# Staged first loads with zero products ahead of them, and last products in eight banks with a mean taken chunk by chunk

## What is computed

```python
h = rmsnorm(x, norm_mix[layer])                     # start: layer 0
z = jax.nn.gelu(h @ w_in)                           # start: first product
...
x = x + moe_swiglu(h, m_w_router[j], ...)           # end: expert rows added to x
return rmsnorm(x, norm_final), new_rows, win_state, jnp.stack(a_states)
```

## Time and profile before

| | us |
|---|---|
| three runs, median (lowest to highest) | 1208.33 (1204.21 to 1209.13) |
| the profiled execution, its own time | 1208.35 |
| its span in the trace | 1206.7 |
| PE busy | 1165.2 (97% of the span) |
| DVE busy | 800.0 |
| ACT busy | 694.8 |
| mean granted TensorE clock, share of full | 0.983 |

### The profile page before, as it was taken

The page is one execution under the profiler, slowest core; times in us unless marked ns, Lnnn a source line. Parts: engine busy times, 40 slices in busy tenths (PEclk is TensorE's granted clock), DMA queues, the critical chain, the costliest instruction groups (busy, mean ns, idle before and its releaser), DMA issues.

```text
span 1206.7 us, 20229 instructions
## 1 busy us (share of the span) xinstructions
PE 1165.2 (97%) x7512; PEld 946.0 (78%) x7512; DVE 800.0 (66%) x1257; ACT 694.8 (58%) x1081; POOL 52.8 (4%) x77
## 2 busy tenths in 40 slices
PE   6999999999999899999999999998999999999987
PEld 6999999999996678854888888655888887887544
DVE  6677666666653976402998997206998998996214
ACT  6666444555547787302887886105887887885011
POOL 1000000000430000100000000000000000000100
PEclk9999999999999899799999999999999999999997
DMA  9574545455666966999999999899999999998992
GB/s 348 185 260 181 200 158 201 158 201 209 236 205 221 384 207 262 410 393 382 420 421 421 392 421 383 346 420 420 420 420 422 421 423 358 404 418 316 389 420 84
DMA packets 69236, 390.36 MB, mean 323 GB/s; under 512 B 6710, under 2 KB 25786, under 8 KB 30682
## 3 DMA queue, kind: packets, MB, share of 16 engines
q1 hardware_dynamic: 64138, 367.44, 76.9%
q0 software_dynamic: 5008, 21.72, 5.0%
HBM read 366.92 MB, written 26.40 MB: 326 GB/s over the span
## 4 chain that ended last, share of the span: by engine, by line
PE 82%; DVE 7%; DMA 5%; ACT 4%; issue 2%; SPq 0%; DVEq 0%; ACTq 0%
PE bank L2229 12%; PE bank L2230 12%; PE bank L2231 12%; PE bank L1733 9%; PE bank L1734 9%; PE bank L1735 8%; PE bank L2180 8%; PE bank L2161 4%; DMA raw<-in_moe 4%; PE bank L2214 1%; DMA ring<-in_wd 1%; ACT arena L865 1%; PE bank L2094 1%; DVE d_lo L1147 1%; DVE w_lo L1582 1%
## 5 line engine op out<-in xcount | busy, mean ns | idle before, releaser
L1582 DVE TENSOR_TENSOR w_lo<-raw,w_hi 128x1024 fp32r<-128x1024 f32 x330 | 394.0, 1220 | 26.1 <-ACT w_hi L984 14.3
L984 ACT CAST w_hi<-raw 128x1024 fp32r<-128x1024 f32 x330 | 340.2, 1055 | 67.2 <-PE bank L2231 52.8
L1147 DVE TENSOR_TENSOR d_lo<-ring,d_hi 128x1024 fp32r<-128x1024 f32 x120 | 147.8, 1237 | 84.9 <-ACT d_hi L736 82.5
L1733 PE MATMUL bank<-hA_hi,d_hi 128*128 128x264 f32 x640 | 184.5, 288 | 12.4 <-DVE hA_lo L1137 9.5
L1734 PE MATMUL bank<-hA_lo,d_hi 128*128 128x264 f32 x640 | 182.4, 285 | 0.0
L1735 PE MATMUL bank<-hA_hi,d_lo 128*128 128x264 f32 x640 | 182.2, 285 | 0.0
L2229 PE MATMUL bank<-w_hi,xg_hi 128*128 128x512 f32 x440 | 172.7, 392 | 2.8 <-DVE w_lo L1582 2.8
L2230 PE MATMUL bank<-w_lo,xg_hi 128*128 128x512 f32 x440 | 172.1, 391 | 0.0
L2231 PE MATMUL bank<-w_hi,xg_lo 128*128 128x512 f32 x440 | 171.9, 391 | 0.0
L736 ACT CAST d_hi<-ring 128x1024 fp32r<-128x1024 f32 x120 | 125.0, 1045 | 77.5 <-PE bank L1735 68.6
L1733 PEld LDWEIGHTS bank<-hA_hi,d_hi 128*128 128x128 f32 x640 | 121.6, 190 | 14.8 <-issue 12.5
(11 more groups left out here) (372 smaller groups left out, 1717.1 us busy)
## 6 DMA issues: line engine op xcount, KB each, us to landing
raw<-in_moe SPq DMA_DIRECT2D x258, 1024.0 KB, 13.5
ring<-in_wd SPq DMA_DIRECT2D x29, 2048.0 KB, 8.1
out_rows<-zeros SPq DMA_DIRECT2D x1, 6656.0 KB
slot_rows<-zeros SPq DMA_DIRECT2D x1, 6144.0 KB
early_units<-in_moe SPq DMA_DIRECT2D x6, 1024.0 KB, 11.2
xs<-slot_rows POOLq DMA_DIRECT2D x5, 512.0 KB, 8.2
out_rows<-yrow POOLq DMA_DIRECT2D x5, 512.0 KB, 8.0
arena<-in_cmp_pages POOLq DMA_DIRECT2D x16, 128.0 KB, 3.2
```

What stands on the lines that cost most here:

```text
L984: nc.scalar.copy(w_hi[:, i % NSPLIT, :], raw[:, raw_slot(u), ITEM * (i % 2):ITEM * (i % 2) + ITEM])\
L1147: V.tensor_tensor(d_lo[:, n % NDS, :], raw_item(n), d_hi[:, n % NDS, :].bitcast(F32), ALU.subtract)\
L1582: V.tensor_tensor(w_lo[:, i % NSPLIT, :], raw[:, raw_slot(i // 2), ITEM * (i % 2):ITEM * (i % 2) + ITEM], w_hi[:, i % NSPLIT, :].bitcast(F ...
L1733: T.matmul(out, w_hi_[:, j, :], hi[:, k, :], start=(first and j == 0), stop=False)
```

## The change

At the start three waits are put between SP's issues: tile v0's rest waits for the second half of x, tile v1 for item 1, the constants and all behind them for tile v1. PE runs twelve matmuls of zeros (256 columns) before the first product. At the end `yrow` is copied in quarters, the eight products get eight banks and follow one another, the pairwise additions of squares are gone, the mean is taken of every chunk, `stay_awake` is gone from this part, and root and reciprocal are one instruction each.

```diff
-        LAST_BANKS = [T0, T1, B[0], B[1], STAT, T0, T1, B[0]]
+        LAST_BANKS = [T0, T1, B[0], B[1], B[3], STAT, MISC, B[2]]
...
             sp.wait_ge(item_in[0], 16)
             sp.dma_start(ring[:, 0, DITEM:2 * DITEM], wd[0][:, DITEM:2 * DITEM]).then_inc(item_in[1], 16)
+            sp.wait_ge(x_in[1], 16)
...
                     sp.dma_start(ring[:, n % NSLOT, first:], wd[wn][:, first:]).then_inc(done, 16)
                     wn += 1
+                if n == 0:
+                    sp.wait_ge(item_in[1], 16)
                 if n == NSLOT - 1:
 
+                    arrived(sp, TILES[n])
                     sp.dma_start(C[:], consts).then_inc(spatial_in, 16)
...
+            pe.wait_ge(zeros_ready, 1)
+            for _ in range(12):
+                T.matmul(MISC[:, 0:256], zeros[:, 0:P], zeros[:, :], start=True, stop=True)
             pe.wait_ge(setup_in, 16)
...
-            nc.scalar.copy(yrow[0:64, 0:512], B[2][0:64, :]).then_inc(left_ready, 1)
+            for half in range(2):
+                nc.scalar.copy(yrow[0:64, 256 * half:256 * half + 256], B[2][0:64, 256 * half:256 * half + 256]).then_inc(left_ready, 1)
...
-            nc.scalar.activation(tok_rstd[:, 0:2], B[2][:, 0:2], ACT.Sqrt, bias=vector("eps")[:, 0:1])
-            nc.scalar.activation(tok_rstd[0:NS, 2:3], B[2][0:NS, 2:3], ACT.Sqrt, bias=vector("eps")[0:NS, 0:1]).then_inc(tok_std, 1)
+            nc.scalar.activation(tok_rstd[:, 0:3], T0[:, 0:3], ACT.Sqrt, bias=vector("eps")[:, 0:1]).then_inc(tok_std, 1)
...
-            V.tensor_copy(yrow[64:128, 0:512], B[2][64:128, :]).then_inc(right_ready, 1)
-            for c in range(KC):
-                add_combined(1, c)
-                if c in (2, 4, 6, 7):
-                    j = c // 2 - 1 if c < 7 else 3
-                    dve.wait_ge(sq_ready, 32 + 2 * j + 2)
-                    V.tensor_tensor(sq_last[:, 2 * j, :], sq_last[:, 2 * j, :], sq_last[:, 2 * j + 1, :], ALU.add).then_inc(sum_step, 1)
+            for half in range(2):
+                V.tensor_copy(yrow[64:128, 256 * half:256 * half + 256], B[2][64:128, 256 * half:256 * half + 256]).then_inc(right_ready, 1)
+            for n in range(KC):
+                add_combined(1, n)
...
-            for c in range(KC):
-                combine(c)
-                if c >= 5:
-                    last_mean(c - 5)
-            last_mean(3)
-            stay_awake(B[3], 3)
-            pe.wait_ge(tok_scale, 4)
+            for n in range(KC):
+                combine(n)
+            for n in range(KC):
+                last_mean(n)
+            pe.wait_ge(tok_scale, 3)
```

More of the change, by code:

```diff
@@ L1690, in _ @@
             dve.wait_ge(yrow_free, wides + (WIDE_STEP + 1))
-            V.tensor_copy(yrow[64:128, 0:512], B[2][64:128, :]).then_inc(right_ready, 1)
-            for c in range(KC):
-                add_combined(1, c)
-                if c in (2, 4, 6, 7):
-                    j = c // 2 - 1 if c < 7 else 3
-                    dve.wait_ge(sq_ready, 32 + 2 * j + 2)
-                    V.tensor_tensor(sq_last[:, 2 * j, :], sq_last[:, 2 * j, :], sq_last[:, 2 * j + 1, :], ALU.add).then_inc(sum_step, 1)
+            for half in range(2):
+                V.tensor_copy(yrow[64:128, 256 * half:256 * half + 256], B[2][64:128, 256 * half:256 * half + 256]).then_inc(right_ready, 1)
+            for n in range(KC):
+                add_combined(1, n)
             dve.wait_ge(tok_std, 2)
-            V.reciprocal(tok_rstd[:, 0:2], tok_rstd[:, 0:2]).then_inc(tok_scale, 1)
-            V.reciprocal(tok_rstd[0:NS, 2:3], tok_rstd[0:NS, 2:3]).then_inc(tok_scale, 1)
+            V.reciprocal(tok_rstd[:, 0:3], tok_rstd[:, 0:3]).then_inc(tok_scale, 1)
             dve.wait_ge(rstd_spread, 1)
@@ L2122, in combine @@
             def combine(n):
[L2124 to L2128, removed]
+                if n in (0, 4):
+                    pe.wait_ge(left_ready, n // 4 + 1)
+                if n in (1, 5):
+                    pe.wait_ge(right_ready, n // 4 + 1)
+                if n == 5:
                     pe.wait_ge(comb_added, KC)
-                if n >= 5:
-                    pe.wait_ge(comb_added, KC + n - 4)
                 c = LAST_ORDER[n]
@@ L2135, in combine, with last_mean @@
                     .then_inc(comb_done, 1)
-            def last_mean(j):
-                stay_awake(B[3], 4 if j == 3 else 1)
-                pe.wait_ge(sum_step, 28 + j + 1)
+            def last_mean(n):
+                pe.wait_ge(sq_ready, 32 + n + 1)
                 for t, (a, z) in enumerate(spans):
-                    i = T.matmul(B[2][0:z - a, t:t + 1], sq_last[:, 2 * j, a:z], mean[:, 0:1], start=(j == 0 and t == 0), stop=(j == 3 and t == 2),
+                    i = T.matmul(T0[0:z - a, t:t + 1], sq_last[:, n, a:z], mean[:, 0:1], start=(n == 0 and t == 0), stop=(n == KC - 1 and t == 2),
                                  skip_group_check=True)
-                if j == 3:
+                if n == KC - 1:
                     i.then_inc(mean_done, 1)
```

## The result

The changed kernel took 1210.26 us in the median of 15 runs (1207.49 to 1214.37), the kernel before 1203.93 in the 15 runs beside it (1200.81 to 1209.13): ratio 1.0057, 95% interval 1.0042 to 1.0072, slower by 5 to 9 us. The forecast was 1204.5, 3.9 us faster than the profiled execution of before. A second set of 12 runs on another occasion gave 1209.85 against 1205.66, ratio 1.0031 (1.0010 to 1.0052).

The account below looks back on a forecast made before the run. PE, busy 97% of the span, was taken as the bound except at its two ends: item 1 and u0's arrival at the start, one token-wise mean at the end. 1208.35 - 0.7 - 3.1 = 1204.5 us, range 1201.6 to 1208.4.

Parts of the forecast that it names:

- Item 1 and product 2: Start: item 1 cast at 11.5 to 12.5 instead of 13.15, product 2 near 18.7 instead of 20.21.
- Zeros: Start of PE: twelve zero matmuls end near 9.8, product 0 then runs at full clock; no gain by itself.
- v1's landing: Start, loads: tile v1 lands at 18.9 instead of about 20.5, part of the engines' lag being gone.
- its 34.8: Start, loads: tile u0 lands at 34.8, as now; the queue loses about 1.8 us empty and regains the lag.
- only one wait finds the queue empty: Start, loads: of the added waits just one meets an empty queue and pays the fixed transfer cost of about 2 us.
- Rival 1: Start: u0 comes late, at 36.6, product 8 at 38.9, +1.0 us against now, time 1206.2; chance 0.2.
- the start term: Start up to product 8, at about 37.15 instead of 37.88: -0.7 us, bounds -1.6 and +1.0.
- The end: From the `yrow` copy to the scaling: -3.1 us, between -0.1 and -5.9; clock falling at about 1192.15 as now.
- -2.2 and -1.0: End: mean done at 1195.3 instead of 1197.53 (-2.2); root to scaling 2.0 instead of 2.99 us (-1.0).

Follow-up runs that it names:

- third_only: Kernel before plus only the wait of the constants and all behind them for tile v1; 1210.64 against 1205.66 us, ratio 1.0037.
- ctrl_after: The changed kernel run once more, nothing altered, against the kernel before; 1209.85 against 1205.66 us, ratio 1.0031.
- waits_only: Kernel before plus only the three waits between the first loads; 1212.83 against 1205.53 us, ratio 1.0049.
- after_filler: Changed kernel plus seven matmuls of zeros ahead of product 8, against the kernel before; 1206.80 against 1205.28 us, ratio 1.0028.
- ctrl_before: The kernel before run once more, nothing altered, against itself; 1202.93 against 1205.66 us, ratio 0.9974.
- tail_only: Kernel before with only the new last part, nothing changed at the start; 1204.04 against 1205.53 us, ratio 0.9982.
- tail_params_late: Kernel before with the new last part and parameters and late vectors issued behind tile u0, no waits or zeros; 1203.77 against 1205.28 us, ratio 0.9994.

## Why the prediction was wrong

The forecast was -3.8 us (-0.7 and -3.1) from the 1208.35 of one execution. In the first set the kernel before had a median of 1203.93, 4.4 us under that base, and the change came out at +6.3. So the change was missed by 10 us and the time by only 5.8, a piece of luck in the base.

**Item 1 and product 2: right.** Cast 11.40 (foreseen 11.5 to 12.5), product 2 at 18.45 (18.7). But the gain was counted against an execution in which item 1 happened to be late. Over the six kernels with the old loads it stands at 11.9, over the five with all three waits (11.40, 11.09, 10.90, 11.97, 11.61) at 11.4: the usual gain is 0.5 us, not 1.7.

**Zeros: right.** They ended at 9.32 (9.8 foreseen), product 0 ran at full clock, and nothing depended on it. Full clock is read here from the rows' lengths (0.28 us where the kernel before had 0.42), since the clock column shows 1.00 in both from 0 us on.

**The step that failed** is this one: "I take v1's landing as 18.9 (average done at 18.2, part of the lag gone since each load starts together)", and behind it "the queue loses about 1.8 us empty and wins back the lag". v1 landed at 20.75, as late as the 20.5 of before; nothing was won back, in none of the five kernels with all three waits (20.75, 19.69, 21.54, 21.61, 21.98), nor in third_only (20.18). In the six kernels with the old loads it landed at 18.4 to 20.5, so the waits made it later if anything. Of the 2.5 us by which u0 missed its 34.8, 1.85 are v1's landing and 0.7 the way from there (16.6 us where 15.9 were counted; 16.6 to 18.1 in the other kernels with this wait and all transfers ahead of u0). The first two waits add holes of their own (item 8 at 36.65 without the third, 35.48 with the first alone), where the prediction had said that only one wait finds the queue empty, and the hole at 20 us is 3.2 us of full rate, not 1.8, since the queue came back to 430 GB/s only over three microseconds (99, 218, 390 GB/s). u0 was there at 37.3 instead of 34.8. Rival 1, given 0.2, had the mechanism, with 36.6 for u0 and +1.0 us; the bound of the start term (+1.0) was too near.

**What no case had** is the clock. I priced PE's wait ahead of product 8 by its length; but after 3.4 us of idle time PE also ran at half speed, 1.6 to 2.8 us more. The Trainium skill (TensorE: Matmul & The Clock Gate, HAM oscillation) describes just this, a wait for a transfer behind which the array is throttled again; I used that page for the end and not here. The traces agree in the changed kernel, ctrl_after and waits_only, with 3.4, 3.6 and 3.8 us idle ahead of product 8, and after_filler, with that time filled, kept the clock; in third_only, with 2.9 us idle, it did not happen.

**The end: near in size by luck, against the execution that was profiled,** -3.6 where -3.1 was forecast (its own parts, -2.2 and -1.0, add up to -3.2). Of the 3.6, 2.0 are the change and 1.6 a clock that happened to fall 7.5 instead of 5.5 us after the copy; the forecast had it fall at the same time as before. Means done 8.0 us after the copy (8.6 foreseen), 48 rows in 5.46 us. Over all traces the old end takes 13.88, 10.36, 12.69, 12.28, 12.97, 12.48 (mean 12.4), the new one 10.32, 10.22, 10.21, 10.51, 11.76, 10.63, 12.22 (mean 10.8): -1.6 us, and -2.0 at the same fall of the clock. That the best of each, 10.36 and 10.21, are near one another does not make the two ends equal: the first had the full clock throughout, the second had it for 7.6 us only, as the spread ahead of the scaling shows (ctrl_before, then tail_only):

```profile
1194.84 1.02 PE L2282 MATMUL bank<-consts_sb,tok_rstd 128*128 128x128 f32 x6
...
1193.21 1.74 PE L2273 MATMUL bank<-consts_sb,tok_rstd 128*128 128x128 f32 x6 [0.56 <-DVE tok_rstd L1696]
```

What the new end takes at full clock no trace shows. I had read one execution's clock as the kernel's.

**The sum.** Item 12 is at 43.69 in the mean of the six kernels with the old loads (44.92, 43.93, 42.84, 43.16, 44.09, 43.18), and at 48.33, 49.41 and 50.52 in those with all three waits and nothing else moved: 49.4, +5.7 us. Start +5.7 and end -2.0 give +3.7, and +4.1 with the mean of the ends, -1.6, where +6.3 and +4.2 were measured in the medians. The second fits; of the first, 2 us stay open. The middle was 1.1 us longer in the mean of the kernels with all three waits (1142.0 against 1140.9), inside its scatter, and the kernel before differs from itself by 2.7.

## What to carry to other kernels

A wait between loads on one queue helps the load ahead of it only if that one is held up by those behind; what it costs is paid by the first load behind the hole that someone waits for, so look for the tile with the least slack further down before putting it in. If that tile is late and can pass loads that nobody needs yet, do that first: with the waits in place one line of order was worth 5 us here. Without them it was worth nothing that can be told, since the tile was in time, and the row of waits was worth less than nothing. Take two or three profiles of a kernel before pricing a change of one or two microseconds against it, and where the clock falls in the part that is priced, compare traces in which it falls at the same time.

## What was not expected of the hardware

A queue that has run dry does not come back at once: after the constants were issued at 20.75, 16 GB/s from 20 to 21 us, 99 in the first whole microsecond, 218 and 390 in the next two, then 430. In third_only, issued at 20.18, it was 192 from 21 to 22 us, 344 and 393.

The landing of tile v1 is late against the bytes by some 2 us, and a wait does not mend it: in third_only the queue moved 49 GB/s from 18 to 20 us and v1 landed at 20.18.

One kernel's executions differ by more than the change: 1198.45 to 1211.34 in 35 runs of before. A part of it sits near 500 us, where the clock is at half for a longer or a shorter time (windows of before, then of after_filler: busy and count of PE, PEld, DVE, ACT, POOL, clock, DMA share, GB/s):

```profile
495.00:520.00 25.00, 24.13 (x145) 18.74 (x147) 7.25 (x46) 3.05 (x6) 6.33 (x7) 0.66 0.99 391
```

```profile
495.00:520.00 25.00, 23.93 (x198) 18.29 (x197) 10.64 (x67) 7.70 (x14) 5.73 (x6) 0.93 1.01 418
```

The second has 198 matmuls in that stretch, the first 145: by (0.93 - 0.66) x 25 = 6.8 us of full clock the two differ. In twelve of the fourteen traces the clock in that stretch is 0.66 to 0.73, in after_filler and tail_params_late 0.93, and these two have the shortest middles (1138.5 and 1137.6 us). No edit touches that stretch; whether the two came there by chance is not shown, with one trace each.
